# Stick-breaking mixer: one ScalarE function set for exponential and logarithm, and the last output products in another order

## The reference

```
def stick_breaking_mix(q, k, v):                  # 12 heads of 64, blocks of 128 tokens
    for blk in range(seq // Q_BLOCK):
        z = einsum(q[block], k[:end]) * scale
        log_keep = where(before, -softplus(z), 0.0)
        later = cumsum(log_keep, reverse=True) - log_keep
        att = where(before, exp(log_sigmoid(z) + later), 0.0)
        out = einsum(att, v[:end])
heads = concatenate([stick_breaking_mix(q, k, v), memory_attention(mq, mem_k, mem_v)])
x = layer_norm(ALPHA * x + heads @ w_out)
```

## Time and profile before

| | us |
|---|---|
| timed runs, median of 3 (lowest, highest) | 1703.74 (1703.65, 1704.11) |
| profiled execution | 1700.73 |
| its span on the core | 1699.4 |
| TensorE busy in the span | 1639.3 (96%) |
| ScalarE busy | 802.6 (47%) |
| VectorE busy | 942.3 (55%) |
| mean granted TensorE clock | 0.98 of full speed |

### The profile page before, as it was taken

How to read it: one execution, slowest core, us unless ns; L and a number is a source line. 1 busy time by engine, 2 the same in 40 slices (tenths; PEclk the granted TensorE clock), 3 DMA queues, 4 the chain that set the end, 5 groups by cost and what they waited for, 6 DMA issues and landing times.

```text
span 1699.4 us, 29823 instructions
## 1 busy us (share of the span) xinstructions
PE 1639.3 (96%) x13094; PEld 1503.6 (88%) x13094; DVE 942.3 (55%) x1199; ACT 802.6 (47%) x1059; POOL 129.6 (8%) x117
## 2 busy tenths in 40 slices
PE   7999999988999999999999989999999999999998
PEld 7999897767999989998998879998999988789997
DVE  6444463445545555445795565546645474575545
ACT  6444444434444454444655254444544456764443
POOL 0000020000000001000376101000020010001000
PEclk9999999879999999999999999999999999999999
DMA  7745443313655445554530066454655542345551
GB/s 275 270 176 195 153 174 150 123 50 125 215 185 188 169 169 203 183 189 149 179 124 4 3 223 223 174 198 149 225 179 193 180 169 98 125 174 199 191 181 75
DMA packets 40865, 280.67 MB, mean 165 GB/s; under 512 B 4794, under 2 KB 4794, under 8 KB 8864
## 3 DMA queue, kind: packets, MB, share of 16 engines
q1 hardware_dynamic: 39024, 272.40, 44.6%
q0 software_dynamic: 1712, 6.37, 1.0%
HBM read 277.14 MB, written 1.08 MB: 164 GB/s over the span
## 4 chain that ended last, share of the span: by engine, by line
PE 90%; DVE 4%; ACT 3%; DMA 2%; issue 1%; SPq 0%; DVEq 0%; ACTq 0%
PE P L231 88%; PE P L242 2%; DMA raw<-ws 1%; ACT whi L205 1%; DMA gb<-gains 1%; DVE wlo L219 1%; DVE xt L279 1%; ACT xt L272 0%; DVE x L359 0%; PE P L2011 0%; DVE AR L791 0%; ACT AR L817 0%; DVE AR L371 0%; DVE AR L1077 0%; DVE AR L2120 0%
## 5 line engine op out<-in xcount | busy, mean ns | idle before, releaser
L231 PE MATMUL P<-xt,whi 128*128 128x256 f32 x5088 | 934.5, 286 | 14.6 <-DVE xt L279 12.1
L231 PEld LDWEIGHTS P<-xt,whi 128*128 128x128 f32 x5088 | 803.8, 193 | 29.3 <-issue 18.3
L231 PE MATMUL P<-xt,wlo 128*128 128x256 f32 x2544 | 702.3, 283 | 0.0
L219 DVE TENSOR_TENSOR wlo<-raw,whi 128x2048 fp32r<-128x2048 f32 x245 | 559.7, 2290 | 80.8 <-PE P L231 76.9
L205 ACT ACTIVATE whi<-raw 128x2048 fp32r<-128x2048 f32 x245 | 467.1, 1908 | 161.2 <-PE P L231 120.2
L231 PEld LDWEIGHTS P<-xt,wlo 128*128 128x128 f32 x2544 | 488.7, 192 | 0.0
L653 DVE TENSOR_TENSOR AR<-P,AR 128x256 f32<-128x256 f32 x114 | 48.4, 425 | 334.6 <-ACT AR L624 334.6
L624 ACT ACTIVATE AR<-P 128x256 f32<-128x256 f32 x114 | 43.7, 384 | 354.3 <-PE P L231 354.3
L231 PE MATMUL P<-whi,hh 128*128 128x512 f32 x504 | 197.5, 392 | 0.0
L231 PE MATMUL P<-wlo,hh 128*128 128x512 f32 x504 | 196.8, 390 | 0.0
L231 PE MATMUL P<-whi,hl 128*128 128x512 f32 x504 | 196.1, 389 | 0.0
(11 more groups left out here) (225 smaller groups left out, 934.8 us busy)
## 6 DMA issues: line engine op xcount, KB each, us to landing
raw<-ws SPq DMA_DIRECT2D x249, 1024.0 KB, 4.8
gb<-gains SPq DMA_DIRECT2D x16, 512.0 KB, 7.3
AR<-by_distance POOLq DMA_DIRECT2D x1, 3072.0 KB, 19.5
x<-x_in SPq DMA_DIRECT2D x2, 512.0 KB, 4.0
AR<-mem_in POOLq DMA_DIRECT2D x1, 1024.0 KB, 5.2
out<-x SPq DMA_DIRECT2D x2, 512.0 KB, 2.6
cs<-cst SPq DMA_DIRECT2D x1, 737.0 KB, 14.1
AR<-cst POOLq DMA_DIRECT2D x1, 420.0 KB, 4.6
```

The lines of the kernel that those rows point to most:

```text
L219: dve.e.tensor_tensor(k.wlo[n % NLO][:, :], k.raw[u % NRAW][:, :], k.whi[n % NHI][:, :].bitcast(F32), ALU.subtract).then_inc(*k.s_lo.inc(u))
L231: return pe.e.matmul(o, l, r, start=start, stop=stop, skip_group_check=True)
```

## The change

Two things change, both in the stick-breaking mixer.

1. At the top of `stick_mixer_scalar` ScalarE is told to load the function set `natural_log_exp_and_others`, which holds the exponential and the logarithm. (The rehearsal, a dry walk that counts semaphores, learns the name of the call.)
2. `out` and `out_tensor` get an argument `of`: which of a unit's two chunks are multiplied. The output products around S4, T5 and S5 are cut in halves of 6 products and put in another order.

```
-    memset = dma_start = then_inc = same
+    memset = dma_start = then_inc = preload_act_table_set = same
...
-def out_tensor(k, pe, u, n, first, part):
+def out_tensor(k, pe, u, n, first, part, of=(0, 1)):
...
-    for i in range(2):
+    for i in of:
...
-    def out(u, n, part):
+    def out(u, n, part, of=(0, 1)):
...
-        last = out_tensor(k, pe, u, n, u == U + 10, part)
-        if part:
+        last = out_tensor(k, pe, u, n, u == U + 10, part, of)
+        if part and of[-1]:
             last.then_inc(*k.s_used.inc(u))
...
     out(U + 10, 0, 1)
+    out(U + 12, 1, 0, (0,))
     stick_sums_tensor(k, pe, 4)
     stick_tensor(k, pe, 5)
-    out(U + 12, 1, 0)
+    out(U + 12, 1, 0, (1,))
+    out(U + 11, 3, 1, (0,))
     stick_sums_tensor(k, pe, 5)
-    out(U + 11, 3, 1)
+    out(U + 11, 3, 1, (1,))
     out(U + 13, 2, 0).then_inc(*k.s_dn.inc("sb", "out"))
     out(U + 12, 1, 1)
     out(U + 13, 2, 1)
...
 def stick_mixer_scalar(k, act):
     U, P, att = U_SB, k.P, k.recall2
+
+    act.e.preload_act_table_set("natural_log_exp_and_others")
```

## The result

| | before, us | after, us |
|---|---|---|
| timed, median (lowest, highest) | 1703.76 (1703.65, 1704.11), 4 runs | 1694.57 (1692.28, 1697.27), 4 runs |
| ratio of the times | | 0.9949, 95% interval 0.9936 to 0.9963 |
| profiled execution | 1700.73 | 1697.27 |
| its span | 1699.4 | 1696.0 |

The two spans lie only 3.4 us apart. Neither number is the effect of the change; the traces show why.

What follows compares the result with a forecast made beforehand. TensorE was taken to bound the kernel, waiting for ScalarE at S2 and S4. Terms -0.92 - 3.07 - 1.41 + 0.1 = -5.3 us took the median from 1703.74 to 1698.4 us, range 1697.2 to 1700.4.

Steps and rivals of the forecast that it cites:

- What bounds the stage, and the two waits: TensorE bounds the mixer; its waits for L2552's exponentials ahead of S2 and S4 go, -0.92 and -3.07 us.
- A load costs ScalarE 1.43 us: ScalarE in the mixer: each load with its broken overlap costs 1.43 us; thirteen go, 18.6 us, nearly all beside TensorE's work.
- The clock term of 1.41 us: S4 and T5: low clock after the 3.07 us wait slows products by 0.68 + 0.73 us; it goes, -1.41 us.
- The new order is worth nothing beside the set, and costs 0.1 us: Output products around S4 to S5: S4 has 1.2 us to spare without the reordering; less cover behind S5 costs 0.1 us.
- Behind S5: Ahead of U + 13's products: six products cover instead of 12, so TensorE waits 0 to 0.2 us, taken as 0.1.
- Rival (a): Behind S5: a wait near 2 us brings low clock back; gain 2.1 us, 1701.6, or 1699.8 if only the clock fails; chance 0.09.
- The joint set's functions cost the same: ScalarE's passes: exponential and logarithm from the joint set take no longer, 0.94 us a pass; at twice that, the sum is -4.9.
- Rival (c): Activations between pair 5's scores and S4: joint set's functions are slow, about +5 us, 1708.7; chance 0.04.
- Rival (b): Last SwiGLU layer: weights do not come earlier, gain is given back and shrinks to 0 to 3 us, 1702.2; chance 0.09.
- I carry this over: From trace to time: the timed median's 3.0 us above the profiled execution stays, so 1703.74 - 5.3 = 1698.4 us.
- for what moves between executions: Range's lower end, 1697.2: 1.2 us below the forecast for differences between executions and a shorter chain than seen.
- lie beside TensorE's work: Loads at L817 and L2512 of pair 0: TensorE waits there for nothing of theirs, so removing them counts nothing.

Runs made afterwards that it cites:

- the run with one load more: Kernel before with the joint set for pairs 0 to 3 only, old set reloaded ahead of pair 4, old product order; mixer's stretch 74.03 us against 74.21.
- the filled wait: Kernel before with 13 unused products added on TensorE in the wait ahead of S4, all loads left; mixer's stretch 72.97 us against 74.21.
- the repeated activations: Changed kernel with four activations repeated in pair 5's first pass, holding ScalarE up about 2.1 us; mixer's stretch 69.21 us.
- the order alone: Changed kernel without the line naming the joint set, so new product order with all 13 loads; ratio to the kernel before 0.9995.
- the start's wait filled: Changed kernel with 8 unused products in TensorE's wait for L484 at the mixer's start, run twice; 1697.29 and 1694.02 us.

## Why the prediction was right or wrong

- **What bounds the stage, and the two waits.** Right. Both waits for L2552 are gone. On the clock of the trace before, S4 was forecast at 1479.7 and S5 at 1485.2; with the mark's 1.95 us taken off they came at 1479.5 and 1485.0. The norm's first addition, forecast near 1490.5, came at 1490.4.
- **A load costs ScalarE 1.43 us.** Right, and the run with one load more showed it from the other side: 1.43 less 0.62 of idleness came out as 0.68 us of wait at S4.
- **The clock term of 1.41 us.** Right as a mechanism: the filled wait took it away alone (1.24 us). In size it holds for five of six executions; in the sixth it was 1.5 us larger, and the sum had no term for that.
- **The new order is worth nothing beside the set, and costs 0.1 us.** Right: 68.66 us without it, 68.75 with it.
- **Behind S5.** Right: under 0.1 us. Rival (a)'s longer wait appeared only where ScalarE was slower (0.5 us with the loads, 0.3 us with the repeated activations), and no low clock followed it.
- **The joint set's functions cost the same.** Right, 0.93 to 0.94 us. Rival (c) is out. Rival (b) too: the last layer showed no new wait, and from L359 to the end it took 203.57 us before and 203.68 after.
- **The step that failed** is the last one, from the trace to the time: "The median of the timed runs stands 3.0 us above that execution; I carry this over", and with it the 1.2 us "for what moves between executions". I took three alike times as a sign that the kernel repeats within 0.3 us, though the profiled execution, 3 us below them, already said otherwise. The 3.0 us were no constant distance but the spread of executions. It measures 2.1 us (standard deviation) before and 2.3 us after, and comes in part with the mean clock. The miss from 1698.4 to 1694.57 us, 3.8 us, falls into three: the first three times before stood 1.0 us above the mean of the many (1702.7); the gain is 6.8 us in the means where 5.3 was summed, 1.5 us; and the first four times after stood 1.3 us below their mean (1695.9). The first and the last are luck of the draw. At a spread of 2.2 us, the distance of a median of three from a median of four has a standard error of about 1.9 us (an estimate from that spread), and 1.2 us was too little for it. Of the 1.5 us, 0.4 lie in the mixer's stretch (5.7 instead of 5.3), 0.2 at L817, and the rest stays open.
- **Two smaller faults:** that the loads at L817 and L2512 of pair 0 "lie beside TensorE's work" holds for the trace that it was read from, and failed in one of six: 1.13 us of wait. And "a clock of 1.00 from 1404 to 1501 us" was wrong even for the first profile, since the low clock at the mixer's start can last until about 1406 us or come later.

In the mixer the change is thus worth 5.5 us in most executions and 7.0 where S4's low clock would have been long (8.1 in the one profile that also waited at L817), and all that the traces show of it is the function set's.

## What to carry to other kernels

Where exponential and logarithm alternate, name the set that holds both; but price it at the waits of the bounding engine and not at the number of loads: here 13 loads of 1.43 us were worth 5.5 us, at two waits. Which loads were hidden depended on the clock here: in one execution TensorE, at full clock, arrived early enough to meet loads that the other five traces show as hidden. The wait of 3.07 us at S4 cost its length and, in low clock behind it, about half as much again. Before a profile's microseconds are added to a median, compare several executions of the unchanged kernel: where they differ by 2 us, a gain of 5 us is right in the trace and still up to 4 us off in the first medians.

## What the runs showed of the hardware

- After a wait of 1.8 to 2.8 us at the mixer's start, a stretch at 1.2 GHz came within 2 us in 14 of the 15 profiles without filling, for 3.4 us in eight and 6.8 us in six. In the fifteenth the clock stayed full there, and 3.4 us at the low clock came 12 us later, about 2 us behind the wait of 1.13 us for L817; which of the two waits it belongs to is not shown. In both profiles with the start's wait filled no low clock came before the mark. After 1.72 us at S4 in the order alone, and after 0.9 us at S2, it did not come; after 3.07 us and more at S4 it always did, at once.
- The low clock depends on the execution and not on the kernel alone: at about 915 us, in the RWKV mixer, one profile had 20.5 us of it in one piece, two others 6.8 us, and the other 14 none there.
